# Block 1's gated feed-forward as seven block products a pair, and one packed transpose in the compressed branch

## The chip, the core and the metric

The kernel runs on one core of a Trainium2 chip. The metric is the device time of one execution in microseconds (us), from the first to the last instruction and the little around them. The engines are TensorE (PE in the rows; its weight loads are PEld), VectorE (DVE), ScalarE (ACT), GpSimd (POOL) and SyncE (SP, which here only issues the weight transfers). All work beside each other and meet through semaphores.

## The reference

Three transformer-like blocks run one after the other on 512 tokens of width 1024, in float32. The change touches block 1 only, in two places.

```python
D_MODEL = 1024; SEQ = 512
D_FF = ((8 * D_MODEL // 3 + 255) // 256) * 256          # 2816 = 22 tiles of 128

# feed-forward at the end of block 1
h = rms_norm(x, norm_ffn_g)
x = x + (jax.nn.silu(h @ w_ffn_gate) * (h @ w_ffn_up)) @ w_ffn_down

# compressed branch of the attention: 31 compressed keys, 16 heads, 4 tiles of 128 queries
s_c = jnp.einsum('bgrqd,bgnd->bgrqn', qb, k_c).astype(jnp.float32) * scale
p_c = masked_softmax(s_c, c_end[None, :] <= tpos[:, None])
o_c = jnp.einsum('bgrqn,bgnd->bgrqd', p_c.astype(dt), v_c)
```

## The kernel before

**Products in three parts.** TensorE multiplies in the rounded type fp32r. For float32 accuracy every operand is held as a high half (rounded to fp32r) and a low half (the rest), and a product is three matmuls: high by high, high by low, low by high (`three`, L2553 to L2557). An activation operand is `HI[...]`, `LO[...]`; a weight operand is `w_hi`, `w_lo`.

**Weights as a stream of units.** A unit is 1024 x 128 weights, 512 KB: eight tiles of 128 x 128, one for each slice of the contraction. Every unit U takes the same way through two buffers, by the parity of U: SyncE loads it into `raw` (loop at L400 and behind), ScalarE rounds it into `w_hi` (`split_hi`, L574 to L578, which waits until TensorE has finished unit U - 2), GpSimd subtracts to get `w_lo` (`low_half`, L429 to L431), TensorE runs 24 matmuls of 128 x 512 on it (`unit`, L2569). `PLANS` lists the stages of a block with their units; all engines go through that list in the same order, and semaphores (`w_loaded`, `w_hi_ready`, `w_lo_ready`, `mm_done`) count units.

**The feed-forward.** D_FF is handled in three parts of 8, 8 and 6 tiles. A stage `ffn_up_q` has two units for each tile, one of `w_ffn_gate` and one of `w_ffn_up`: a *pair*, 22 in all. `scaled_pairs` (TensorE, L2612) multiplies, each unit into its own PSUM bank. `scaled_operands` (VectorE, L1702 to L1720) scales the gate by the norm's factor `stat[:, 1]` (L1708), ScalarE applies Silu (L742), VectorE scales up (L1711), multiplies the two (L1714), rounds the hidden tile into its high half (L1718) and subtracts for the low half (L1720). A stage `ffn_down_q` then multiplies the hidden tiles by eight units of `w_ffn_down` (`single`, L2660), and VectorE adds the result to `X` (`residual_add`, L1664). The norm's factor itself comes late: `residual_add_operand` (L1686 to L1696) adds the attention's output to `X` unit by unit in stage `attn_out`, makes the operand (unscaled by the norm) and sums squares; TensorE starts `ffn_up_0` with it before the factor is there (`fresh=True`).

**The compressed branch.** For each head `transposes` (L2853 to L2867) turns four tiles of compressed probabilities (128 queries x 32) with one transpose each (L2862), ScalarE copies them out of PSUM (L975, L976), and `values` (L2882) multiplies each by the compressed values.

## Time and profile before

| | us |
|---|---|
| median of three timed runs | 2816.99 (2815.65 to 2817.27) |
| profiled execution | 2814.94 |
| its span, first to last instruction | 2813.2 |
| TensorE busy | 2719.2 (97%) |
| VectorE / ScalarE / GpSimd busy | 57% / 36% / 42% |
| FFN of block 1 (`ffn_up_0` to `ffn_down_2`) | about 670 to 1048 of the span |

A busy share counts instructions in flight, so for TensorE, whose matmuls overlap, the distance between the starts of two matmuls says more than the share. A row of the timeline gives the start, the duration, the engine, the line, the operation with output and inputs and their shape, and in brackets how long the engine sat idle before it and which engine's instruction ended that. An instruction's duration includes time in which it was started but blocked.

### The profile page before, as it was taken

How to read it: one execution, taken by the hardware profiler on the slowest of the kernel's cores; microseconds unless marked ns; L12 is line 12 of the kernel's file. 1: busy time of each engine (PE TensorE's matmuls, PEld its weight loads, DVE VectorE, ACT ScalarE, POOL GpSimd, SP SyncE). 2: the span in 40 equal slices, each digit the busy share in tenths (PEclk: the TensorE clock that was granted, in tenths of full speed). 3: DMA queues.
4: the chain of work that ended last, by engine and by line, in shares of the span. 5: the costliest groups of instructions: out<-in, count | busy, mean ns of one | idle time of the engine just before them, and what ended most of it. 6: DMA issues, size and time to landing. Idle time of an engine off the chain costs nothing.

```text
span 2813.2 us, 38287 instructions
## 1 busy us (share of the span) xinstructions
PE 2719.2 (97%) x13208; PEld 2244.6 (80%) x13208; DVE 1590.6 (57%) x2560; ACT 1023.4 (36%) x1775; POOL 1178.3 (42%) x592
## 2 busy tenths in 40 slices
PE   8999999999999999999999999999899999999998
PEld 6877888778888877878887788888677778888886
DVE  8996767574433376466665745536623447643364
ACT  4225655533222254443324411112525553211124
POOL 3442585234444443354423344444342214444443
PEclk9999999999999999999999999999999999999999
DMA  3342000132223233222112332232231112322332
GB/s 140 98 135 83 16 24 9 46 127 99 97 93 98 93 120 100 83 87 72 54 38 85 130 101 97 97 96 92 93 105 61 46 45 95 122 97 97 97 97 90
DMA packets 67460, 242.90 MB, mean 86 GB/s; under 512 B 7771, under 2 KB 10116, under 8 KB 66572
## 3 DMA queue, kind: packets, MB, share of 16 engines
q1 hardware_dynamic: 59760, 215.37, 23.3%
q10 hardware_dynamic: 7580, 25.91, 2.6%
q8 instruction: 78, 1.28, 0.2%
q14 instruction: 42, 0.34, 0.0%
HBM read 232.80 MB, written 6.35 MB: 85 GB/s over the span
## 4 chain that ended last, share of the span: by engine, by line
issue 46%; PE 36%; POOL 14%; DVE 2%; ACT 1%; POOLq 0%; DMA 0%; DVEq 0%; SPq 0%; ACTq 0%
POOL w_lo L431 12%; PE bank L2555 9%; PE bank L2557 9%; PE bank L2556 9%; PE bank L3109 2%; PE bank L3098 2%; PE bank L2880 1%; POOL stat L458 1%; POOL stat L455 1%; PE bank L2770 1%; PE bank L2867 0%; PE bank L2741 0%; DVE big L1904 0%; PE bank L2828 0%; PE bank L2829 0%
## 5 line engine op out<-in xcount | busy, mean ns | idle before, releaser
L431 POOL TENSOR_TENSOR w_lo<-raw,w_hi 128x1024 fp32r<-128x1024 f32 x398 | 972.9, 2445 | 1566.5 <-ACT w_hi L578 1446.0
L2555 PE MATMUL bank<-act,w_hi 128*128 128x512 f32 x3128 | 1258.4, 402 | 54.1 <-POOL w_lo L431 16.4
L2557 PE MATMUL bank<-act,w_lo 128*128 128x512 f32 x3128 | 1226.3, 392 | 0.0
L2556 PE MATMUL bank<-act,w_hi 128*128 128x512 f32 x3128 | 1225.0, 392 | 0.0
L2555 PEld LDWEIGHTS bank<-act,w_hi 128*128 128x128 f32 x3128 | 591.5, 189 | 203.4 <-issue 34.6
L578 ACT CAST w_hi<-raw 128x1024 fp32r<-128x1024 f32 x396 | 415.7, 1050 | 906.7 <-PE bank L2557 884.9
L2557 PEld LDWEIGHTS bank<-act,w_lo 128*128 128x128 f32 x3128 | 591.3, 189 | 126.8
L2556 PEld LDWEIGHTS bank<-act,w_hi 128*128 128x128 f32 x3128 | 592.6, 189 | 120.6 <-issue 5.5
L1664 DVE TENSOR_TENSOR X<-X,bank 128x512 f32 x56 | 38.5, 688 | 241.3 <-PE bank L2557 241.3
L2046 DVE CAST act<-tmp 128x512 f32 x64 | 140.9, 2202 | 10.0 <-DVE tmp L2042 5.2
L1816 DVE SCALAR_TENSOR_TENSOR bank<-big,cols,bank 128x512 f32<-128x512 f32 x174 | 117.1, 751 | 0.4
L2880 PE MATMUL bank<-big 128*128 128x64 f32 x640 | 82.1, 276 | 12.9 <-DVE big L1917 12.7
L2880 PEld LDWEIGHTS bank<-big 128*128 128x128 f32 x640 | 77.6, 194 | 17.2 <-issue 14.6
L963 ACT ACTIVATE tmp<-bank,big 128x128 f32<-128x128 f32 (+3 forms) x128 | 66.8, 531 | 41.0 <-DVE big L1904 34.9
L1904 DVE TENSOR_REDUCE big<-bank 128x2 f32<-128x256 f32 (+1 forms) x64 | 52.7, 823 | 45.8 <-PE bank L2830 45.6
L458 POOL TENSOR_TENSOR stat<-stat 128x512 f32<-128x512 f32 x58 | 74.1, 1277 | 4.8
L1711 DVE TENSOR_TENSOR tmp<-bank,stat 128x512 f32<-128x512 f32 x22 | 15.2, 692 | 104.9 <-PE bank L2557 104.9
L973 ACT COPY big<-bank 128x128 f32<-128x128 f32 (+3 forms) x128 | 48.3, 431 | 55.1 <-PE bank L2867 55.0
L2446 DVE SCALAR_TENSOR_TENSOR big<-bank,stat 128x128 f32<-128x128 f32 (+3 forms) x32 | 15.7, 491 | 91.0 <-ACT stat L1389 91.0
L2221 DVE TENSOR_TENSOR stat<-bank,cst 128x256 f32<-128x256 f32 x96 | 40.8, 425 | 39.9 <-PE bank L3098 38.1
L1692 DVE TENSOR_TENSOR X<-X,bank 128x512 f32<-128x512 f32 x24 | 16.5, 688 | 78.8 <-PE bank L2557 73.5
L3098 PEld LDWEIGHTS bank<-big 128*128 128x128 f32 x384 | 50.6, 192 | 12.7 <-ACT big L1199 4.2
(427 smaller groups left out, 2967.3 us busy)
## 6 DMA issues: line engine op xcount, KB each, us to landing
raw<-in_w_dram SPq DMA_DIRECT2D x402, 512.0 KB, 3.5
act_f<-head_rows ACTq DMA_DIRECT2D x8, 768.0 KB, 4.7
proj_rows<-big ACTq DMA_DIRECT2D x4, 1024.0 KB
big<-proj_rows ACTq DMA_DIRECT2D x2, 2048.0 KB, 10.0
X<-in_x_dram SPq DMA_DIRECT2D x4, 512.0 KB, 6.0
act_f<-in_cw1k_dram ACTq DMA_DIRECT2D x4, 512.0 KB, 4.2
cst<-in_consts_dram ACTq DMA_DIRECT2D x2, 648.5 KB, 8.9
X<-big ACTq DMA_DIRECT2D x8, 128.0 KB, 3.2
```

Of the source, the lines that this page charges most:

```text
L431: pool.tensor_tensor(w_lo[:, u], raw[:, u].rearrange("p (k n) -> p k n", k=KT), w_hi[:, u].bitcast(F32), ALU.subtract).then_inc(w_lo_ready, 1)
L458: pool.tensor_tensor(to, acc, product, ALU.add).then_inc(done, 1)
L578: a.copy(w_hi[:, u].rearrange("p k n -> p (k n)"), raw[:, u]).then_inc(w_hi_ready, 1)
L963: a.activation(by_tile(tmp[:, 2 * b + j, 0:kw]), score_branches(n)[:, j], ACT.Exp, bias=MX[:, b, j:j + 1], accum_out=SUMS[:, n % 4, j:j + ...
L1816: v.scalar_tensor_tensor(acc, src, w, acc, ALU.mult, ALU.add).then_inc(conv_tap, 1)
L2046: v.tensor_copy(hi, y).then_inc(hi_made, 1)
L2555: pe.matmul(o, l_hi, r_hi, start=start, stop=False)
L2556: pe.matmul(o, l_hi, r_lo, start=False, stop=False)
L2557: return pe.matmul(o, l_lo, r_hi, start=False, stop=stop)
L2880: pe.matmul(o[:, j], PT[:, b, j, k * P:k * P + P], V_TOK[:, 2 * j + g // 2, k, (g % 2) * DH:(g % 2) * DH + DH], start=k == 0, stop=k == qt)
L3098: ins = pe.matmul(bank[2 + half][:, quad[j]], MT[:, 2 * half + j], TM[:, 2 * half + j], start=True, stop=True)
L3109: ins = pe.matmul(bank[4 + half][:, quad[j]], XM[:, 2 * half + j], UM[h % 2][:, 2 * half + j], start=True, stop=True)
```

## The change

**Seven products.** The pair of gate and up units with its operand is taken as a 2 x 2 block matrix product: rows are gate and up, the contraction is split in slices 0 to 3 and 4 to 7, and the 512 tokens in two halves N1 and N2 of 256. Instead of eight block products (4 slices, 256 tokens, three matmuls each: 12 matmuls of 128 x 256) seven are made. For that:

- A pair's seven weight operands are A11 and A12 (the gate unit, cast and subtracted as before), A22 (half of the up unit) and four sums S_1, S_2, S_4, S_3. VectorE forms the sums (`mix_weights`, four instructions of 512 elements in SBUF), ScalarE rounds A22 and the sums (`split_piece`, five casts of 512), GpSimd makes their low halves (five subtractions of 512). `PIECES = 6` counts them: one whole unit and five halves.
- The operand's mixed forms MIXED_1 to MIXED_4 are made once, in stage `attn_out` (`residual_add_mixed_operand` in place of `residual_add_operand`).
- TensorE writes the products to five banks (A to E); ScalarE keeps the first product in SBUF (`keep_first_product`); VectorE combines the banks to gate and up in seven instructions of 256 elements, and scales.
- The rounding of the hidden tile goes from VectorE to ScalarE (`high_hidden`).
- SyncE loads the next pair's two units once the sums of this pair are made (`loads_behind_pair`). The bytes loaded are the same.
- The adding of `ffn_down_q` is written out, with the first sums of the next stage ahead of its last unit.

**Packed compressed branch.** The four tiles of 32 probabilities a head lie side by side (`PC_ROWS`, 128 x 128) and take one transpose and one copy of 128 columns in place of four transposes and two copies (384 and 128). The values stand in `VC_T` four times, once for each tile at its own 32 rows with zeros elsewhere.

The diff, cut to its core (lines of `@@` name the engine; the semaphore renames and the counters are left out):

```diff
@@ plan and storage @@
     ("attn_out", 8),
-    ("ffn_up_0", 16), ("ffn_down_0", 8), ("ffn_up_1", 16), ("ffn_down_1", 8), ("ffn_up_2", 12), ("ffn_down_2", 8)],
+    ("ffn_up_0", 48), ("ffn_down_0", 8), ("ffn_up_1", 48), ("ffn_down_1", 8), ("ffn_up_2", 36), ("ffn_down_2", 8)],
...
+SEVENTHS = ("ffn_up_0", "ffn_up_1", "ffn_up_2")
+PIECES = 6
...
+        MIXED_1 = HI[B][:, 0:4, N2], LO[B][:, 0:4, N2]
...
+        def slots(F):
+            other = 1 - F % 2
+            return OWN_SLOTS + [(w_hi[:, other, k:k + 4], w_lo[:, other, k:k + 4]) for k in (0, 4)]
+        def split_from(F):
+            return [RAW_W[:, 1 - F % 2, 4:8]] + [SUMS_W[:, n] for n in range(4)]
...
@@ SyncE @@
+def loads_behind_pair(F, L, M, j):
+    sp.wait_ge(weights_mixed, M + 4 * j + 4)
+    for n in range(2):
+        u = (L + n) % 2
+        sp.wait_ge(w_lo_ready, F + PIECES * j + 1 + n)
+        sp.dma_start(raw[:, u], t["w"][L + 2 * j + 2 + n]).then_inc(w_loaded[u], 16)
...
@@ GpSimd @@
+    from_unit = rest + 9
+    for F, L, M, n in SEVEN.values():
+        halves_between(from_unit, F)
+        with pool.Fori(0, n) as j:
+            low_half(F + PIECES * j, F % 2)
+            for k, ((hi, lo), src) in enumerate(zip(slots(F), split_from(F))):
+                pool.wait_ge(w_hi_ready, F + PIECES * j + k + 2)
+                pool.tensor_tensor(lo, src, hi.bitcast(F32), ALU.subtract).then_inc(w_lo_ready, 1)
+        from_unit = F + PIECES * n
+    halves_between(from_unit, heads)
...
@@ ScalarE @@
+def split_piece(stage, j, k):
+    F, L, M, n = SEVEN[stage]
+    if k == 0:
+        a.wait_ge(w_loaded[1 - F % 2], loaded(L, 1) + 16 * j)
+    else:
+        a.wait_ge(weights_mixed, M + 4 * j + k)
+    if isinstance(j, int) and j == 0:
+        if k >= 3:
+            a.wait_ge(mm_done, F)
+    else:
+        a.wait_ge(mm_done, F + PIECES * j - PIECES + SLOT_FREE[k])
+    a.copy(slots(F)[k][0], split_from(F)[k]).then_inc(w_hi_ready, 1)
...
+    def keep_first_product(j, begun=False):
+        a.wait_ge(mm_done, F + PIECES * j + 1)
+        if not begun:
+            a.wait_ge(dve_read, used + 7 * j - 2)
+        a.copy(P1_KEPT, BANK_A).then_inc(act_read, 1)
+    def high_hidden(j):
+        a.wait_ge(full_made, full + j + 1)
+        a.copy(HI[A][:, bass.ds(j, 1), :].rearrange("p a t -> p (a t)"), tmp[:, 3]).then_inc(hi_made, 1)
+    def next_unit(j):
+        u = F % 2
+        a.wait_ge(w_loaded[u], loaded(L, 2) + 16 * j)
+        a.wait_ge(mm_done, F + PIECES * j + 3)
+        a.copy(w_hi[:, u].rearrange("p k n -> p (k n)"), raw[:, u]).then_inc(w_hi_ready, 1)
+    def silu(j):
+        a.wait_ge(gate_scaled, scaled + j + 1)
+        a.activation(tmp[:, 2], tmp[:, 2], ACT.Silu).then_inc(act_read, 1)
+    def rest(j):
+        next_unit(j)
+        for k in range(4):
+            split_piece(name, j + 1, k)
+        silu(j)
+        split_piece(name, j + 1, 4)
...
@@ VectorE @@
+def mix_weights(name, j, k):
+    F, L, M, n = SEVEN[name]
+    first, second = RAW_W[:, F % 2], RAW_W[:, 1 - F % 2]
+    to = SUMS_W[:, k]
+    if k == 0:
+        for x in range(2):
+            v.wait_ge(w_loaded[(L + x) % 2], loaded(L, x) + 16 * j)
+    v.wait_ge(w_lo_ready, F - 1 if isinstance(j, int) and j == 0 else F + PIECES * j - PIECES + k + 3)
+    if k in (1, 2):
+        v.wait_ge(weights_mixed, M + 4 * j + k)
+    one, two = ((second[:, 0:4], second[:, 4:8]), (SUMS_W[:, 0], first[:, 0:4]), (SUMS_W[:, 1], first[:, 4:8]),
+                (first[:, 0:4], second[:, 0:4]))[k]
+    v.tensor_tensor(to, one, two, ALU.add).then_inc(weights_mixed, 1)
...
+def residual_add_mixed_operand(name, block, gain, dst, stage):
...
+        if k < 4:
+            at = made + 2 * k
+            v.tensor_tensor(MIX[:, 4], X[:, k, N1], X[:, k, N2], ALU.subtract).then_inc(full_made, 1)
+            low(LO[dst][:, k, N1], HI[dst][:, k, N1], X[:, k, N1], g(k), at + 1)
+            v.wait_ge(full_made, full + k + 1)
+            low(MIXED_1[1][:, k], MIXED_1[0][:, k], MIX[:, 4], g(k), at + 2)
+        else:
+            i, at, done = k - 4, made + 8 + 4 * (k - 4), full + 4 + 3 * (k - 4)
+            link(v.tensor_scalar(MIX[:, 0], X[:, k, N2], g(k), None, ALU.mult))
+            v.scalar_tensor_tensor(MIX[:, 1], X[:, i, N2], g(i), MIX[:, 0], ALU.mult, ALU.subtract).then_inc(full_made, 1)
+            v.wait_ge(full_made, done + 1)
+            v.scalar_tensor_tensor(MIX[:, 2], X[:, i, N1], g(i), MIX[:, 1], ALU.mult, ALU.subtract).then_inc(full_made, 1)
+            v.wait_ge(full_made, done + 2)
+            v.scalar_tensor_tensor(MIX[:, 3], X[:, k, N1], g(k), MIX[:, 2], ALU.mult, ALU.subtract).then_inc(full_made, 1)
+            low(MIXED_3[1][:, i], MIXED_3[0][:, i], MIX[:, 1], None, at + 2)
+            v.wait_ge(full_made, done + 3)
+            low(MIXED_4[1][:, i], MIXED_4[0][:, i], MIX[:, 3], None, at + 4)
+            low(LO[dst][:, k], HI[dst][:, k], X[:, k], g(k), at + 1)
+            low(MIXED_2[1][:, i], MIXED_2[0][:, i], MIX[:, 2], None, at + 3)
+        if k < KT - 2:
+            add_square(k)
+    mix_weights(stage, 0, 1)
+    add_square(KT - 2)
+    add_square(KT - 1)
+    mix_weights(stage, 0, 2)
+    mix_weights(stage, 0, 3)
...
+    def pair(j, last=False):
+        step = lambda k: v.wait_ge(dve_read, used + 7 * j + k)
+        mix = (lambda k: None) if last else lambda k: mix_weights(name, j + 1, k)
+        mix(0)
+        v.wait_ge(mm_done, F + PIECES * j + 3)
+        v.tensor_tensor(gate[:, N1], BANK_A, r[:, N1], ALU.mult).then_inc(dve_read, 1)
+        mix(1)
+        v.wait_ge(mm_done, F + PIECES * j + 4)
+        v.wait_ge(act_read, reads + 2 * j + 1)
+        v.tensor_tensor(U_PART, P1_KEPT, BANK_B, ALU.subtract).then_inc(dve_read, 1)
+        step(2)
+        v.tensor_tensor(U_PART, U_PART, BANK_C, ALU.add).then_inc(dve_read, 1)
+        mix(2)
+        v.wait_ge(mm_done, F + PIECES * j + 5)
+        step(3)
+        v.tensor_tensor(gate[:, N2], U_PART, BANK_E, ALU.add).then_inc(dve_read, 1)
+        step(4)
+        v.tensor_tensor(gate[:, N2], gate[:, N2], r[:, N2], ALU.mult).then_inc(gate_scaled, 1)
+        mix(3)
+        v.wait_ge(mm_done, F + PIECES * j + 6)
+        v.tensor_tensor(V_PART, BANK_B, P1_KEPT, ALU.subtract).then_inc(dve_read, 1)
+        step(5)
+        v.tensor_tensor(up[:, N1], V_PART, BANK_D, ALU.add).then_inc(dve_read, 1)
+        v.tensor_tensor(up[:, N2], V_PART, BANK_C, ALU.subtract).then_inc(dve_read, 1)
+        step(7)
+        v.tensor_tensor(up, up, r, ALU.mult).then_inc(dve_step, 1)
+        v.wait_ge(dve_step, steps + j + 1)
+        v.wait_ge(act_read, reads + 2 * j + 2)
+        v.tensor_tensor(up, up, gate, ALU.mult).then_inc(full_made, 1)
+        v.wait_ge(full_made, full + j + 1)
+        v.wait_ge(hi_made, made + j + 1)
+        hi = HI[dst][:, bass.ds(j, 1), :].rearrange("p a t -> p (a t)")
+        lo = LO[dst][:, bass.ds(j, 1), :].rearrange("p a t -> p (a t)")
+        v.tensor_tensor(lo, up, hi.bitcast(F32), ALU.subtract).then_inc(lo_made, 1)
...
@@ TensorE @@
+    A11, A12, A22, S_1, S_2, S_4, S_3 = unit_parts + slots(F)
+    B11, B21, B22 = (hi[:, 0:4, N1], lo[:, 0:4, N1]), (hi[:, 4:8, N1], lo[:, 4:8, N1]), (hi[:, 4:8, N2], lo[:, 4:8, N2])
...
+    def product(o, w, x, begin=True, made=None):
+        for k in range(4):
+            if made is not None:
+                pe.wait_ge(lo_made, base + made(k))
+            ins = three(o, w[0][:, k], w[1][:, k], x[0][:, k], x[1][:, k], begin and k == 0, k == 3, skip_group_check=True)
+        return ins
+    def pair(j, begun=False, fresh=False):
+        def piece(k):
+            pe.wait_ge(w_lo_ready, F + PIECES * j + k)
+        def free(k):
+            if not begun:
+                pe.wait_ge(dve_read, used + 7 * j - 7 + k)
+        def fifth():
+            piece(4 if fresh else 3)
+            free(7)
+            product(BANK_C, S_1, MIXED_1, made=(lambda k: 2 * k + 2) if fresh else None)
+        piece(1)
+        free(1)
+        product(BANK_A, A11, B11, made=(lambda k: 2 * k + 1) if fresh else None).then_inc(mm_done, 1)
+        if fresh:
+            fifth()
+        piece(2)
+        free(6)
+        product(BANK_D, A22, MIXED_4, made=(lambda k: 8 + 4 * k + 2) if fresh else None).then_inc(mm_done, 1)
+        pe.wait_ge(act_read, reads + 2 * j + 1)
+        product(BANK_A, A12, B21, begin=False, made=(lambda k: 8 + 4 * k + 3) if fresh else None).then_inc(mm_done, 1)
+        if fresh:
+            sum_squares()
+        else:
+            fifth()
+        piece(4)
+        product(BANK_B, S_2, MIXED_2, made=(lambda k: 8 + 4 * k + 4) if fresh else None).then_inc(mm_done, 1)
+        piece(5)
+        product(BANK_E, S_4, B22).then_inc(mm_done, 1)
+        piece(6)
+        pe.wait_ge(dve_read, used + 7 * j + 2)
+        product(BANK_B, S_3, MIXED_3, begin=False).then_inc(mm_done, 1)
...
@@ compressed branch: TensorE, ScalarE @@
-            for q in range(TT):
-                to = bank[0][:, P + q * P:2 * P + q * P] if q < 3 else bank[6][:, P:2 * P]
-                pe.transpose(to, PC[:, q], ident)
+            pe.transpose(bank[0][:, P:2 * P], PC_ROWS, ident)
...
-        pe.matmul(o[:, 2], PCT[:, h % 2, qt * P:qt * P + P], VC_T[:, g * DH:(g + 1) * DH],
+        pe.matmul(o[:, 2], PCT[:, h % 2], VC_T[:, qt, g * DH:(g + 1) * DH],
...
-            a.copy(PCT[:, h % 2, 0:3 * P], bank[0][:, P:4 * P])
-            a.copy(PCT[:, h % 2, 3 * P:4 * P], bank[6][:, P:2 * P]).then_inc(c_kept, 1)
+            a.copy(PCT[:, h % 2], bank[0][:, P:2 * P]).then_inc(c_kept, 1)
```

What the change moves on three engines, from the instruction streams of both kernels:

VectorE, the loop over the pairs of `ffn_up_0`, before (ISA and REGISTER_ALU are address and counter work of the loop; `tmp` holds gate and up, `stat` the normalising factor):

```order
L1708 TENSOR_TENSOR tmp<-bank,stat 128x512 [waits mm_done]
L1709 REGISTER_ALU
L1710 REGISTER_ALU [waits mm_done]
L1711 TENSOR_TENSOR tmp<-bank,stat 128x512 [waits lo_made]
L1712 REGISTER_ALU
L1713 REGISTER_ALU [waits act_read]
L1714 TENSOR_TENSOR tmp<-tmp 128x512 [waits dve_read]
L1715 REGISTER_ALU
L1718 ISA [waits full_made]
L1718 COPY act<-tmp 128x512
```

The same loop now, its first half (`raw` and `big` in L1885 are weights and weight sums in SBUF, `big<-big,bank` combines a kept product with a PSUM bank):

```order
L1885 TENSOR_TENSOR big<-raw 128x512 [waits w_lo_ready]
L1945 ISA
L1946 TENSOR_TENSOR tmp<-bank,stat 128x256 [waits mm_done]
L1880 REGISTER_ALU
L1882 ISA [waits w_lo_ready]
L1885 TENSOR_TENSOR big<-big,raw 128x512 [waits weights_mixed]
L1948 REGISTER_ALU
L1949 ISA [waits mm_done]
L1950 TENSOR_TENSOR big<-big,bank 128x256 [waits act_read]
L1942 ISA
L1952 TENSOR_TENSOR big<-big,bank 128x256 [waits dve_read]
```

and its end, behind the last product of the pair:

```order
L1963 TENSOR_TENSOR tmp<-big,bank 128x256 [waits dve_read]
L1964 TENSOR_TENSOR tmp<-big,bank 128x256
L1942 REGISTER_ALU
L1966 TENSOR_TENSOR tmp<-tmp,stat 128x512 [waits dve_read]
L1967 REGISTER_ALU
L1968 REGISTER_ALU [waits dve_step]
L1969 TENSOR_TENSOR tmp<-tmp 128x512 [waits act_read]
L1970 REGISTER_ALU
L1971 REGISTER_ALU [waits full_made]
L1974 ISA [waits hi_made]
L1974 TENSOR_TENSOR act<-tmp,act 128x512
```

Five instructions a pair have become fifteen; eight of them read two operands in SBUF (four L1885, L1958 on `tmp` and `stat`, L1966, L1969, L1974). The cast of L1718 has left this engine.

GpSimd, the loop that makes the low halves of these weights. Before, one instruction a unit:

```order
L431 TENSOR_TENSOR w_lo<-raw,w_hi 128x1024 [waits w_hi_ready]
L435 UNCONDITIONAL_BRANCH
L435 ISA
L431 TENSOR_TENSOR w_lo<-raw,w_hi 128x1024 [waits w_hi_ready]
L430 REGISTER_ALU
```

and now, a pair:

```order
L509 TENSOR_TENSOR w_lo<-raw,w_hi 128x1024 [waits w_hi_ready]
L608 REGISTER_ALU
L609 TENSOR_TENSOR big_r<-raw,big_r 128x512 [waits w_hi_ready]
L608 REGISTER_ALU
L609 TENSOR_TENSOR big_r<-big,big_r 128x512 [waits w_hi_ready]
L608 REGISTER_ALU
L609 TENSOR_TENSOR big_r<-big,big_r 128x512 [waits w_hi_ready]
L608 REGISTER_ALU
L609 TENSOR_TENSOR w_lo<-big,w_hi 128x512 [waits w_hi_ready]
L608 REGISTER_ALU
L609 TENSOR_TENSOR w_lo<-big,w_hi 128x512 [waits w_hi_ready]
```

Two instructions of 1024 elements a pair have become one of 1024 and five of 512.

ScalarE, the same loop. Before, the gate's Silu and a weight cast follow one another; now the first rows of an iteration are:

```order
L827 ISA [waits mm_done]
L828 COPY big<-bank 128x256 [waits dve_read]
L831 REGISTER_ALU
L832 ISA [waits full_made]
L832 COPY act<-tmp 128x512
L836 ISA
L837 REGISTER_ALU [waits w_loaded_odd]
L838 CAST w_hi<-raw 128x1024 [waits mm_done]
```

The cast of the next pair's weights (L838) stands behind L832, which waits for VectorE's last but one instruction of the pair before (`full_made`).


## Rows read from the trace of the kernel before

**Rows 1.** The page: busy time of each engine, share of the span, instructions.
```profile
PE 2719.2 (97%) x13208; PEld 2244.6 (80%) x13208; DVE 1590.6 (57%) x2560; ACT 1023.4 (36%) x1775; POOL 1178.3 (42%) x592
```

**Rows 2.** Busy time in the stretch of `ffn_up_1`; columns length, PE, PEld, DVE, ACT, POOL.
```profile
801.00:889.00 88.00, 88.00 (x390) 72.87 (x389) 42.63 (x42) 21.05 (x24) 40.91 (x17) 1.00 0.29 96
```

**Rows 3.** Timeline (start, duration, engine, line, operation, idle before): two pairs of `ffn_up_0`.
```profile
700.66 0.69 DVE L1711 TENSOR_TENSOR tmp<-bank,stat 128x512 f32<-128x512 f32 x1 [4.84 <-PE bank L2557]
...
701.39 0.69 DVE L1714 TENSOR_TENSOR tmp<-tmp 128x512 f32<-128x512 f32 x1
...
701.71 2.63 POOL L431 TENSOR_TENSOR w_lo<-raw,w_hi 128x1024 fp32r<-128x1024 f32 x1 [1.80 <-ACT w_hi L578]
...
702.22 2.40 DVE L1718 CAST act<-tmp 128x512 f32 x1
...
711.54 0.69 DVE L1711 TENSOR_TENSOR tmp<-bank,stat 128x512 f32<-128x512 f32 x1 [4.84 <-PE bank L2557]
```

**Rows 4.** Timeline: matmuls of 256 columns in a stream, and the four small transposes, in the attention.
```profile
338.50 0.60 PE L2862 MATMUL bank<-cst,big 128*128 128x128 f32 x4
338.94 0.38 PE L2867 MATMUL bank<-cst,tmp 128*128 128x128 f32 x2
...
339.62 0.28 PE L2828 MATMUL bank<-act,big_r 128*128 128x256 f32 x1
339.73 0.28 PE L2829 MATMUL bank<-act,big_r 128*128 128x256 f32 x1
339.85 0.28 PE L2830 MATMUL bank<-big_r 128*128 128x256 f32 x1
339.96 1.22 PE L2880 MATMUL bank<-big 128*128 128x64 f32 x10
```

**Rows 5.** Timeline: VectorE and GpSimd side by side in stages `conv_out` and `attn_out`.
```profile
587.69 2.39 POOL L431 TENSOR_TENSOR w_lo<-raw,w_hi 128x1024 fp32r<-128x1024 f32 x1 [4.23 <-ACT w_hi L578]
587.71 2.92 DVE L1995 TENSOR_TENSOR big<-big,X  x1
...
620.66 0.69 DVE L1995 TENSOR_TENSOR big<-big,X  x1
...
644.83 2.43 POOL L431 TENSOR_TENSOR w_lo<-raw,w_hi 128x1024 fp32r<-128x1024 f32 x1 [3.02 <-ACT w_hi L578]
...
644.91 0.69 DVE L1487 TENSOR_TENSOR bank<-bank,tmp 128x512 f32<-128x512 f32 x1
```

**Rows 6.** Groups of instructions by line and shape: count, busy us, mean ns, idle before.
```profile
L458 POOL TENSOR_TENSOR stat<-stat 128x512 f32<-128x512 f32 x58 | 74.1, 1277 | 4.8
L490 POOL TENSOR_TENSOR stat<-stat,big 128x512 f32<-128x512 f32 x7 | 7.4, 1052 | 0.5
L2221 DVE TENSOR_TENSOR stat<-bank,cst 128x256 f32<-128x256 f32 x96 | 40.8, 425 | 39.9 <-PE bank L3098 38.1
L578 ACT CAST w_hi<-raw 128x1024 fp32r<-128x1024 f32 x396 | 415.7, 1050 | 906.7 <-PE bank L2557 884.9 <-DMA raw<-in_w_dram 11.6 <-issue 9.4
L827 ACT CAST act<-big 128x512 fp32r<-128x512 f32 x8 | 4.9, 616 | 9.1 <-DVE big L1741 8.9
```

**Rows 7.** Timeline: the last unit of `attn_out` on VectorE, and the norm's factor behind it.
```profile
665.40 0.69 DVE L1692 TENSOR_TENSOR X<-X,bank 128x512 f32<-128x512 f32 x1 [3.48 <-PE bank L2557]
...
667.27 0.75 DVE L1696 SCALAR_TENSOR_TENSOR act<-X,cols,act 128x512 fp32r<-128x512 f32 x1
...
673.28 0.69 DVE L1708 TENSOR_TENSOR tmp<-bank,stat 128x512 f32<-128x512 f32 x1 [1.55 <-ACT stat L603]
```

**Rows 8.** Timeline of TensorE where `ffn_down_0` waits for its last hidden tile.
```profile
759.30 0.39 PE L2557 MATMUL bank<-act,w_lo 128*128 128x512 f32 x1
759.90 0.50 PE L2555 MATMUL bank<-act,w_hi 128*128 128x512 f32 x1 [0.21 <-DVE act L1720]
```

**Rows 9.** Busy time in a stretch of the attention, columns as in rows 2.
```profile
300.00:450.00 150.00, 144.29 (x1052) 132.05 (x1053) 99.64 (x284) 84.30 (x266) 123.08 (x116) 0.99 0.05 15
```

**Rows 10.** Busy time at the end of the attention; the column behind POOL is the granted TensorE clock.
```profile
515.00:520.00 5.00, 3.53 (x18) 3.37 (x18) 2.49 (x7) 0.00 (x0) 1.75 (x1) 0.61 0.32 105
```

246 lines of the change are left out of this document (203 added, 43 removed).

## Prediction

> **What bounds the kernel now.** I read the page first: TensorE is busy 97% of the span, no other engine over 57% [rows 1]. The busy time in stretches says the same of the stages that change: 88.0 of 88.0 us in `ffn_up_1`, with VectorE at 43 and GpSimd at 41 [rows 2]. The timeline gives the step. L1711 reads the up unit of a pair at 700.66 and of the next at 711.54: a pair takes 10.88 us, which over its 48 matmuls of 512 columns is 226.7 ns each [rows 3]. So these stages are bound by matmuls, and fewer matmul columns are worth time exactly as long as no other engine needs more than the new TensorE time for a pair.
>
> **TensorE's side.** Matmuls of 256 columns start at 339.62, 339.73, 339.85 and 339.96, so 113 ns apart [rows 4]: half of 226.7, nothing is lost by halving. A pair becomes 7 x 12 x 113 ns = 9.5 us, 1.36 us less, and over 22 pairs 30 us could be won.
>
> **The other engines for one pair.** GpSimd has one subtraction of 1024 at 2.39 alone [rows 5] and five of 512. None of 512 on weights stands in the trace; L458, two plain operands, took 1.28, L490, with one operand repeated, 1.05 [rows 6]. I take 1.28, since these operands are plain too: 2.39 + 5 x 1.28 = 8.8 us. That alone would fit in 9.5. ScalarE: 1.05 for the unit, six casts of 512 at 0.62 [rows 6], and as an estimate 0.4 and 0.6 for the kept product (256) and Silu (512), 5.8 us: it fits. VectorE: seven instructions of 512 at 0.69, eight of 256 at 0.42 [rows 3, 6], 8.2 us, and 0.04 to 0.14 us between two of them in a loop (701.39 starts 0.04 behind the end of L1711, 702.22 starts 0.14 behind that of L1714 [rows 3]), so 9 to 10 us: just about TensorE's new time.
>
> **But VectorE and GpSimd exclude each other.** This is the row on which the forecast rests. L1995 adds two SBUF operands. Alone it took 0.69; begun 0.02 us behind a GpSimd subtraction of 2.39 it took 2.92, and ended 0.55 us behind it [rows 5]. An add with one PSUM operand, begun 0.08 behind such a subtraction, took its 0.69 [rows 5]. The other way round, the subtraction begun at 701.71 beside L1714 took 2.63 in place of 2.39 and ended 2.26 behind L1714's end [rows 3]. The cast L1718 was blocked as well, 2.40 us, in every pair [rows 3]; it goes to ScalarE, so one victim leaves. Eight new or remaining ones stand in the pair: four weight sums, gate by factor (256), up by factor, up by gate, the low half. What each holds exclusively is the time that it ended behind the other: 0.55 for 512 elements, so 0.28 for 256; on GpSimd 2.26 and, less the same 0.13 at the start, 1.15. The sum is 2.26 + 5 x 1.15 + 7 x 0.55 + 0.28 = 12.1 us a pair. **That is more than the 10.88 of today.** Before, the two engines had one such blocked stretch in 10.88 us and it cost nothing, since TensorE did not wait for it.
>
> The Trainium skill, "SBUF — State Buffer", section "Who interferes with whom", says that VectorE's second read port is GpSimd's only one, that it is taken for a whole instruction, and that a VectorE instruction with two SBUF inputs, but not one with a single one, contends with a GpSimd instruction that reads SBUF. By that rule, the trace agrees in both directions, and the rule speaks against this change.
>
> **The steady pair.** 12.1 needs the port never idle. It will be idle, for the engines also wait in a ring. ScalarE's program puts the cast of the next pair's unit behind `high_hidden`, which waits for up by gate of the pair before. From one up by gate to the next: the high half 0.62 and the unit's cast 1.05 (1.7); GpSimd's six subtractions, 8.8, between which VectorE gets three of its weight sums and the gate's scaling in, 3 x 0.55 + 0.28 = 1.9; then up by factor, blocked behind GpSimd's last one, 0.55, and up by gate, 0.69. Sum 13.6, and 0.2 for the hand-overs: **13.8 us a pair**, 2.9 more than before. From both sides: 12.1 by the port alone; 15.0 if VectorE's gaps of up to 0.14 fall on the ring each time. I take 13.8, as the ring is written so in the program and the gap of 0.04 is as frequent as that of 0.14. TensorE then works 9.5 of 13.8 us.
>
> 22 pairs x 2.92 = 64 us. The first pair of a stage finds its weights made in the stage ahead, and the last makes none for a successor; I take 1.2 us off for each of these six: **+57 us** (bounds +20 and +85).
>
> **Around the pairs.** In `attn_out` VectorE's work for each of the last four units grows: the add 0.69, one scaling of 0.3, six instructions of 256 at 0.42, one of 512 at 0.75, the sum of squares 0.69, so 5.0 us, eight of them with two SBUF operands, and in each unit of 5.44 us (24 x 226.7 ns) GpSimd holds the port for 2.4. VectorE so falls some 2 us a unit behind, 8 us at the last, where before its last low half was done under 3 us behind the last add's start (665.40 to 668.0), and the factor was applied at 673.28 [rows 7]. TensorE's first two products need only the first four slices and cover 2.3 us. I take **+7 us**, bounds 2 and 15.
>
> At the start of each `ffn_down`, the cast of its second unit stands behind the last `high_hidden`. From the last product on: five VectorE instructions 2.6 and gaps 0.3, the high half 0.62, the cast 1.05, GpSimd 2.40 and one blocked 0.55, so 7.5 us, against the 5.44 us that the first down unit takes. That is 2 us of waiting in place of the about 0.4 of today (759.30 to 759.90, less one step of 0.23 [rows 8]): three times 1.7, **+5 us**, bounds 0 and 8. Within the down stages I cost the written-out add at nothing: it is one add of 0.69 in 5.44 us, and the four sums before the last one (2.8 us, up to 5 if blocked) still end within a unit.
>
> In the attention TensorE is busy 144.3 of 150 us [rows 9]. Four small transposes take 338.50 to 338.94, 0.11 us each [rows 4]; three of four go, for 16 heads: 48 x 0.11 = **-5 us**, bounds 0 and -8 (ScalarE is also relieved of a copy a head).
>
> **Sum.** 57 + 7 + 5 - 5 = +64 us on the profiled execution's 2814.9, so 2879. The median of the timed runs stands 2.1 us above that execution: 2881.
>
> **The rivals.**
>
> *A, the ring at the shared port (the forecast), slower.* 12.1 to 15.0 us a pair, with the other terms at their ends: +24 to +104, 2841 to 2921. Chance 0.73.
>
> *B, the block costs less than its sum*, because GpSimd's short subtractions leave gaps which VectorE uses without a loss, or take 1.05. Then VectorE's own work bounds, 10.3 us a pair: 22 x -0.6 = -13, + 7 + 5 - 5: about 2811, between 2800 and 2830. For it: GpSimd's 1.05 exists [rows 6]. Against it: every overlap of two SBUF operands that I looked at was a full block. Chance 0.10.
>
> *C, the other side: faster.* All three helpers stay below TensorE's 9.5 us a pair, 22 x -1.36 = -30, + 7 + 3 - 5: 2792. It decides itself where port and ring together come to less than 9.5 us; by the sum above they miss this by 2.6. It holds if the instructions that VectorE issues now do not need GpSimd's port, as the one with a PSUM operand did not [rows 5]. Chance 0.09.
>
> *D, TensorE's clock.* With gaps in every pair the granted clock may fall. Where TensorE was busy 3.5 of 5 us in the attention's end the grant was 0.61 [rows 10]: for most of that stretch the lower level, 1.2 GHz. If some 3 us of every second pair ran so, 1.5 us each would be added, 11 x 1.5 = 16, and more in `attn_out`: 2895 to 2940. For it: 9.5 of 13.8 us is no higher a share than 3.5 of 5. Against it: products wait singly, never for much over 2 us. Chance 0.08.
>
> That the change does less than it says can be left aside: the instruction streams show all seven products and one transpose a head.
>
> **How the numbers follow.** The likeliest case is A, 2881. For 8 in 10 I need A and a part of D, and a little of B: 2830 to 2925. Outside are C, most of B and the top of D. A measurement of this kernel can tell about 0.2%, 5.6 us, from no change. Faster by more: C and a third of B, 0.12. Within: 0.05. Slower: A, D and the rest, 0.83.
>
> **What would show it.** Right: the starts of the first matmul of two pairs lie 12.1 to 15 us apart; weight sums (L1885) average well over 0.69 and some 1.5 us or more; GpSimd's 512 subtractions average over 1.28; TensorE is busy about 70% in `ffn_up_1`, waiting mostly for VectorE reading a bank or for GpSimd's low halves. Wrong: pairs at 9.5 to 10.9 us, weight sums at 0.69 beside a running subtraction. The attention should be 5 us shorter, and the wait ahead of the first gate scaling some 7 us longer. I would be wrong in size if the ring is cut, for instance if ScalarE's cast of the next unit finds `full_made` long reached.

## The result, and the profile after

The changed kernel takes **2896.4 us** (median), the kernel before 2816.8 us beside it: ratio 1.0285, 95% interval 1.0267 to 1.0303, so 80 us slower. 2881 was predicted, with a range of 2830 to 2925. The profiled execution has a span of 2893.2 us against 2813.2. All ratios here are of undisturbed executions; one of a later kernel (copies and operands in PSUM) took 8088 us in the slow state and is left out of its ratio.

The busy time of the whole span on the page, then a stretch of 112 us over `ffn_up_1`, which before took 88 us [rows 2]; its columns are start and end, length, then busy time of PE, PEld, DVE, ACT and POOL, granted clock, DMA share, GB/s:

```profile
PE 2724.6 (94%) x13952; PEld 2284.2 (79%) x13952; DVE 1772.4 (61%) x2816; ACT 1084.6 (37%) x1908; POOL 1290.1 (45%) x680
...
832.00:944.00 112.00, 90.85 (x674) 88.35 (x673) 91.65 (x114) 42.20 (x69) 80.28 (x47) 0.92 0.22 76
```

Before, TensorE never stopped there [rows 2]. Now it is idle for 21 of 112 us, while VectorE is busy for 92 (43 before) and GpSimd for 80 (41). VectorE's work by line, from 675 to 1070 us of the changed kernel (busy us, mean ns, then idle time ahead of the group and what ended it):

```profile
L1885 DVE TENSOR_TENSOR big<-raw 128x512 f32<-128x512 f32 x43 | 63.7, 1482 | 14.0 <-DMA raw<-in_w_dram 12.2 <-ACT stat L698 1.8
L1885 DVE TENSOR_TENSOR big<-big,raw 128x512 f32<-128x512 f32 x43 | 58.8, 1367 | 0.4
L1966 DVE TENSOR_TENSOR tmp<-tmp,stat 128x512 f32<-128x512 f32 x21 | 33.7, 1606 | 0.7
L1958 DVE TENSOR_TENSOR tmp<-tmp,stat 128x256 f32<-128x256 f32 x21 | 21.2, 1010 | 0.7
...
L1974 DVE TENSOR_TENSOR act<-tmp,act 128x512 f32 (+1 forms) x21 | 14.5, 693 | 19.1 <-ACT act L832 19.1
...
L1950 DVE TENSOR_TENSOR big<-big,bank 128x256 f32<-128x256 f32 x21 | 8.7, 415 | 16.4 <-PE bank L2883 16.4
```

The weight sums (L1885), two SBUF operands, average 1.37 and 1.48 us where 0.69 is their own time; the two scalings (L1966, L1958) 1.61 and 1.01 where 0.69 and 0.42 would do. The low half (L1974) has two SBUF operands as well but took 0.69: GpSimd was idle by then. All that read a bank, as L1950, took their plain 0.41 to 0.42. GpSimd in the same stretch:

```profile
L509 POOL TENSOR_TENSOR w_lo<-raw,w_hi 128x1024 fp32r<-128x1024 f32 x38 | 94.9, 2501 | 132.8 <-ACT w_hi L838 81.0 <-ACT w_hi L673 51.8
L609 POOL TENSOR_TENSOR big_r<-big,big_r 128x512 fp32r<-128x512 f32 x43 | 69.2, 1630 | 4.6 <-ACT big_r L789 4.6
L609 POOL TENSOR_TENSOR w_lo<-big,w_hi 128x512 fp32r<-128x512 f32 x44 | 64.0, 1469 | 6.5 <-ACT w_hi L789 6.5
```

Its subtractions of 512 take 1.47 to 1.63 in place of 1.28. And this is whom TensorE waited for from 625 to 1130 us (total, times, longest; the four largest):

```profile
PE bank L2881 <- DVE tmp L1963: 37.2, 19, 2.7
PE bank L2881 <- DVE big L1950: 18.0, 10, 3.1
PE bank L2881 <- POOL big_r L609: 10.9, 1, 10.9
PE bank L2881 <- POOL w_lo L509: 7.8, 6, 3.0
```

The period of a pair shows in the first bank read, L1946. One row gives the eight of `ffn_up_0` (duration in ns as smallest, median and largest, then the first and the last start):

```profile
L1946 DVE TENSOR_TENSOR tmp<-bank,stat x8: 416/418/420, 685.2 to 782.4; 128x256 f32<-128x256 f32 x8
```

Seven intervals in 97.2 us are 13.9 us each, where the kernel before had 10.88 [rows 3]. "Interval" below is always this mean over the seven intervals of `ffn_up_0`. The last of the seven is shorter, since the last pair makes no sums for a successor: 12.9 us here against 14.0 in the mean of the other six, and in later kernels down to 7.9. Where that misleads, the text says so.

Where the 80 us of span went, by TensorE's first matmul of each stage in both traces: up to `attn_out` -4.0; `attn_out` +1.6; `ffn_up_0`, `_1`, `_2` +34.3, +24.9, +19.2 (some 9.4 of the first belong to its first pair, which waits 10.9 us for GpSimd); the starts and ends of the three down stages +1.1, +1.1, +4.0; the rest -2.2.

### The profile page after: what moved, and what is told of

Read it like the earlier page. It is cut to its first block, busy times and chain, and to the rows that moved or that the text cites. A ratio compares the mean times of both kernels' runs of the same rounds, so it can differ in the third digit from the quotient of the medians.

```text
span 2893.2 us, 41013 instructions
## 1 busy us (share of the span) xinstructions
PE 2724.6 (94%) x13952; PEld 2284.2 (79%) x13952; DVE 1772.4 (61%) x2816; ACT 1084.6 (37%) x1908; POOL 1290.1 (45%) x680
## 3 DMA queue, kind: packets, MB, share of 16 engines
q8 instruction: 80, 1.31, 0.2%
## 4 chain that ended last, share of the span: by engine, by line
issue 48%; PE 32%; POOL 17%; DVE 2%; ACT 1%; POOLq 1%; DMA 0%; DVEq 0%; SPq 0%; ACTq 0%
POOL w_lo L509 11%; PE bank L2881 8%; PE bank L2883 7%; PE bank L2882 7%; POOL big_r L609 2%; POOL w_lo L609 2%; PE bank L3494 2%; PE bank L3483 2%; PE bank L3265 1%; POOL stat L544 1%; POOL stat L541 1%; PE bank L3157 0%; PE bank L3252 0%; DVE big L1885 0%; DVE big L2218 0%
## 5 line engine op out<-in xcount | busy, mean ns | idle before, releaser
L509 POOL TENSOR_TENSOR w_lo<-raw,w_hi 128x1024 fp32r<-128x1024 f32 x376 | 918.0, 2442 | 1519.3 <-ACT w_hi L673 1317.8
L2881 PE MATMUL bank<-act,w_hi 128*128 128x512 f32 (+1 forms) x3040 | 1200.8, 395 | 60.6 <-POOL w_lo L509 21.7
L2883 PE MATMUL bank<-act,w_lo 128*128 128x512 f32 (+1 forms) x3040 | 1168.1, 384 | 0.0
L2882 PE MATMUL bank<-act,w_hi 128*128 128x512 f32 (+1 forms) x3040 | 1167.2, 384 | 0.0
L2881 PEld LDWEIGHTS bank<-act,w_hi 128*128 128x128 f32 x3040 | 581.6, 191 | 195.5 <-issue 34.4
L673 ACT CAST w_hi<-raw 128x1024 fp32r<-128x1024 f32 x352 | 369.6, 1050 | 820.0 <-PE bank L2883 808.9
L2882 PEld LDWEIGHTS bank<-act,w_hi 128*128 128x128 f32 x3040 | 581.3, 191 | 107.5 <-issue 5.5
L3265 PEld LDWEIGHTS bank<-big 128*128 128x128 f32 x640 | 76.6, 192 | 19.5 <-issue 15.5
L2881 PE MATMUL bank<-big_r 128*128 128x256 f32 x176 | 55.8, 317 | 37.2 <-DVE tmp L1963 37.2
L1885 DVE TENSOR_TENSOR big<-raw 128x512 f32<-128x512 f32 x44 | 65.5, 1489 | 14.0 <-DMA raw<-in_w_dram 12.2
L609 POOL TENSOR_TENSOR big_r<-big,big_r 128x512 fp32r<-128x512 f32 x44 | 70.6, 1624 | 5.9 <-ACT big_r L789 5.9
L2881 PEld LDWEIGHTS bank<-big_r 128*128 128x128 f32 x176 | 36.9, 210 | 41.4 <-DVE tmp L1963 41.2
```

The lines of the kernel that those rows point to most:

```text
L509: pool.tensor_tensor(w_lo[:, u], raw[:, u].rearrange("p (k n) -> p k n", k=KT), w_hi[:, u].bitcast(F32), ALU.subtract).then_inc(w_lo_ready, 1)
L609: pool.tensor_tensor(lo, src, hi.bitcast(F32), ALU.subtract).then_inc(w_lo_ready, 1)
L673: a.copy(w_hi[:, u].rearrange("p k n -> p (k n)"), raw[:, u]).then_inc(w_hi_ready, 1)
L1885: v.tensor_tensor(to, one, two, ALU.add).then_inc(weights_mixed, 1)
L2881: pe.matmul(o, l_hi, r_hi, start=start, stop=False, **group)
L2882: pe.matmul(o, l_hi, r_lo, start=False, stop=False, **group)
```

## Experiments

My theory was the prediction's: VectorE and GpSimd exclude each other when VectorE has two SBUF operands, and the pair's period is a ring through these blocked instructions. Rivals: VectorE's own in-order work, the port being simply full, the clock, or one more ring.

### The packed compressed branch alone

```
the kernel before, with  PCT = region(2 * P),  VC_T with a copy of the values for each quarter,
one pe.transpose of PC_ROWS a head; the feed-forward untouched
```

> The kernel before with the packed compressed branch alone, full result. From the two traces: the attention and what lies ahead of it ended 4.0 us earlier after the change, and nothing else of this part touches the feed-forward. Theory: 2816.8 - 4 = 2812.8 us (ratio 0.9986). Rival: the 4 us come from elsewhere (VectorE's shorter attention, another order of the weight loads), then no change, 2816.8.

Measured: 2811.2 us against 2815.7, ratio 0.9985 (0.9976 to 0.9994). The stretch of the attention from 272 to 520 us in this run:

```profile
272.00:520.00 248.00, 230.02 (x1692) 209.43 (x1691) 174.91 (x491) 138.63 (x439) 141.55 (x130) 0.99 0.06 18
```

The kernel before has 1724 matmuls there and 233.03 us, 1692 and 230.03 in the changed kernel. This half of the change is worth -4.6 us as a kernel by itself; the rest of the 80 us, some 84, is the other half's.

### Four of the eight operands into PSUM

```diff
-                gate, up, r = tmp[:, 2], tmp[:, 3], stat[:, 1]
+                gate, up, r = tmp[:, 2], bank[7], stat[:, 1]
+                gate_2 = bank[6][:, S // 2:S]
```

> The changed kernel with up, and the second half of gate, kept in PSUM; full result. Four VectorE instructions of a pair (gate by factor, up by factor, up by gate, the low half) then have only one operand in SBUF. Theory (port shared with GpSimd, and the ring through it): 3 x 0.55 + 0.28 = 1.9 us a pair leave the ring, 14.1 becomes 12.2 to 12.6, the whole 2896 - 22 x 1.7 = 2858 us, and the blocked durations of these four fall from 1.6, 0.8, 0.7 us to their own 0.69 and 0.42. Rival, VectorE's own in-order time bounds or TensorE's waits for its banks bound: the number and the sizes of the instructions are unchanged, so the pair stays at 14.0 us and the whole at 2894.

```profile
L1885 DVE TENSOR_TENSOR big<-raw 128x512 f32<-128x512 f32 x43 | 67.5, 1570 | 31.4 <-DMA raw<-in_w_dram 29.7 <-ACT stat L698 1.8
...
L1967 DVE TENSOR_TENSOR bank<-bank,stat 128x512 f32<-128x512 f32 x22 | 15.4, 700 | 0.8
```

2874.1 us, 22 less; interval 12.4 in place of 13.9. Up by factor fell from 1.61 to 0.70 us, as theory had it, but the gain is 1.0 us a pair and not 1.7. (The interval flatters it: its last is 9.25 us, and the other six have a mean of 13.0, also 1.0 less than before the edit.) The first row above shows one reason: VectorE now waits 29.7 us for weight loads (12.2 in the changed kernel). Another is on ScalarE: its cast of the next unit waited for TensorE 9 times in the changed kernel and 19 times here, in each case from 690 to 1072 us:

```profile
ACT w_hi L838 <- PE bank L2883: 9.3, 9, 1.3
ACT w_hi L838 <- PE bank L2884: 13.8, 19, 1.1
```

Other things came late as soon as this was early.

### The cast ahead of the high half

```diff
                 def rest(j):
                     next_unit(j)
+                    high_hidden(j - 1)
...
                     v.tensor_tensor(gate[:, N1], BANK_A, r[:, N1], ALU.mult).then_inc(dve_read, 1)
                     mix(1)
+                    low_hidden(j - 1)
```

> The changed kernel with two instructions in another order, full result: ScalarE casts the next pair's unit before the high half of the hidden row, and VectorE's low half of pair j-1 stands behind the second weight sum of pair j. The work on every engine and at the port is the same. Theory (ring, as in the prediction): GpSimd's first subtraction starts without waiting for up by gate, the ring falls by 0.62 and by what of the 1.05 of the cast now lies beside VectorE's tail; 12.5 to 13.2 us a pair, 2896 - 22 x 1.3 = 2868 us. Rival, the port itself is full: nothing is taken from it, the pair stays at 14.0 and the whole at 2894. Rival, the moved low half now delays the sums and the bank reads behind it: slower than 2896.

```profile
L1886 DVE TENSOR_TENSOR big<-raw 128x512 f32<-128x512 f32 x42 | 63.4, 1511 | 40.0 <-DMA raw<-in_w_dram 27.9 <-issue 10.8 <-ACT stat L698 1.4
...
L1947 DVE TENSOR_TENSOR act<-tmp,act 128x512 f32 (+1 forms) x19 | 31.6, 1663 | 4.8 <-ACT act L832 4.8
```

2907.6 us: 11 slower where 28 faster was expected. Three things are seen. The low half, 0.69 us while GpSimd was idle, stands behind the second sum now and takes 1.66. The sums wait 27.9 us for loads. And the cast that was to come earlier now waits for TensorE, 47.0 us in 17 of 20 cases, since it overwrites the weights of the third product (`mm_done`):

```profile
ACT w_hi L838 <- PE bank L2892: 47.0, 17, 4.5
```

**The ring of the prediction is not the only one.** The changed kernel's own timeline shows a second and a third (start, length):

```profile
848.44 1.77 DVE L1885 TENSOR_TENSOR big<-raw 128x512 f32<-128x512 f32 x1
...
850.51 0.92 SPq L487 DMA_DIRECT2D raw<-in_w_dram  x2
...
851.37 1.41 DVE L1966 TENSOR_TENSOR tmp<-tmp,stat 128x512 f32<-128x512 f32 x1
852.90 0.69 DVE L1969 TENSOR_TENSOR tmp<-tmp 128x512 f32<-128x512 f32 x1
853.74 0.62 ACT L832 CAST act<-tmp 128x512 f32 x1 [2.60 <-DVE tmp L1969]
854.30 1.05 ACT L838 CAST w_hi<-raw 128x1024 fp32r<-128x1024 f32 x1
...
855.43 2.40 POOL L509 TENSOR_TENSOR w_lo<-raw,w_hi 128x1024 fp32r<-128x1024 f32 x1 [3.20 <-ACT w_hi L838]
...
855.55 2.82 DVE L1885 TENSOR_TENSOR big<-raw 128x512 f32<-128x512 f32 x1 [0.32 <-DMA raw<-in_w_dram]
...
865.73 0.39 PE L2881 MATMUL bank<-big_r 128*128 128x256 f32 x1 [2.15 <-DVE tmp L1963]
866.32 0.41 PE L2882 MATMUL bank<-big_r 128*128 128x256 f32 x1
866.53 0.41 PE L2883 MATMUL bank<-big_r 128*128 128x256 f32 x1
...
868.47 0.62 ACT L832 CAST act<-tmp 128x512 f32 x1 [2.59 <-DVE tmp L1969]
870.40 1.05 ACT L838 CAST w_hi<-raw 128x1024 fp32r<-128x1024 f32 x1 [1.31 <-PE bank L2883]
```

In the first pair shown two chains leave the fourth sum's end at 850.21. One goes over VectorE's tail, the high half and the unit's cast to GpSimd's start at 855.43. The other goes over the load of the next two units: issued 850.51, since the fourth sum is the last reader of their buffers, landed by 855.5, when the first sum starts. They are equally long to 0.1 us, so a cut in one gives little. In the next pair a third chain ends last: VectorE's read of bank D (L1963) releases TensorE's second product at 865.73, and the unit's cast waits for the end of the third, until 870.40, 1.31 us behind the high half. TensorE runs at its lower clock there (matmuls 0.21 us apart, where 0.12 is usual).

### Both edits, and half of the loads

> Both edits of the two runs ahead: up and half of gate in PSUM, and the cast of the next unit ahead of the high half; full result. Port's sum by the prediction's terms 12.1 - 1.9 = 10.2 us, ring cut. Theory: 10.5 to 11.5 us a pair, 2896 - 22 x 3.1 = 2828 us, still not under the 2816.8 of before. Rival, if one edit already did all (they cut the same wait): 12.4 us a pair, 2860. If seven products could win at all, the pair would come under 10.88.

2884.9 us, interval 13.2: 57 us over the expected 2828 and 11 worse than the first edit alone, as the new order cost 11 us in the run ahead too. The blocked low half is not what costs this: it takes 0.68 us here. The sums wait 46.2 us for loads, and the unit's cast waits for TensorE in 19 cases, 45.9 us. The next two runs load half of each unit inside the loops (stale weights in the other half), on the changed kernel and on this one:

```diff
-                    sp.dma_start(raw[:, u], t["w"][L + 2 * j + 2 + n]).then_inc(w_loaded[u], 16)
+                    sp.dma_start(raw[:, u, 0:4 * P], t["w"][L + 2 * j + 2 + n][:, 0:4 * P]).then_inc(w_loaded[u], 16)
```

> The changed kernel, but in the loops over pairs each weight load brings only the first 512 of a unit's 1024 columns; the others keep stale weights, so the products' numbers are others. Question: is there a second ring through the loads (fourth weight sum, load issued, 5.0 us to the landing, first sum), as long as the one of the prediction (fourth sum, up by factor, up by gate, high half, unit's cast)? In the trace after, sum four ended 850.21, the loads were issued 850.51, and the next pair's first sum waited for the landing until 855.55, while ScalarE's unit cast, behind the high half, ended 855.35. Theory, twin rings of the same length: the load's half alone wins little, 14.1 becomes 13.8 to 14.0, and with shorter first pairs the whole is 2896 - 6 = 2890 us. Rival, the loads alone bound: 2.4 us less a pair, 2843. Rival, no ring of loads: 2895.

> The kernel with up and half of gate in PSUM and the unit's cast moved ahead of the high half (2884.9 us, pairs of 12 and 15.6 us, VectorE waiting 46 us for loads), and half loads as before (stale weights in the other half). Theory, twin rings: here the ring over the high half is cut and the loads are what is left; with half of the load time gone the pair falls to 11 to 12 us, 2885 - 22 x 2.0 = 2841 us, much more than the same edit gives in the run beside this one. Rival, the port or VectorE's own time bounds: 2880.

Measured 2891.2 us (-5, interval 13.6) and 2840.5 us (-44, interval 11.3), each a single run. What the edit does to a load, issue to landing from 690 to 780 us in the changed kernel (KB each, median us), first whole, then half:

```profile
raw<-in_w_dram SPq DMA_DIRECT2D x14, 512.0 KB, 3.9
raw<-in_w_dram SPq DMA_DIRECT2D x14, 256.0 KB, 2.8
```

The same edit gives over eight times as much where the other order was in. So the loads alone do not bound the changed kernel, and they do stand in the second one. Two limits: the changed kernel's runs spread over 8 us, so its -5 does not by itself tell 2890 from the 2895 of no ring. And the -44 is more than the loads' own part: an interval is 1.9 us shorter, a load 1.1 (both loads together some 1.4), and the four sums, which now stand less behind GpSimd's subtractions, took 1.4 us less a pair (means 1.32 to 1.05 and 1.71 to 1.28). The loads matter there also by when the sums start.

### The weight sums off the port

```diff
+                if apart:
+                    two = bank[7].rearrange("p (k n) -> p k n", k=4)
                 v.tensor_tensor(to, one, two, ALU.add).then_inc(weights_mixed, 1)
```

> The changed kernel with the second operand of the weight sums of pairs 2 to n-1 read from a bank that holds zeros: the sums are of the same size and in the same places, but have one operand in SBUF (numbers of the products are others). Theory, port: the sums' durations fall from 1.4 mean to 0.69 and GpSimd's subtractions from 1.5 to 1.3 or less; 4 x 0.55 = 2.2 us leave the ring; 16 of the 22 pairs have it: 14.1 becomes 12.0 to 12.6, 2896 - 16 x 1.8 = 2867 us. Rival, the block is not what sets the pair (VectorE's issue and order, TensorE's waits): durations fall, the pair stays at 14, 2893 us.

```profile
L1887 DVE TENSOR_TENSOR big<-big,bank 128x512 f32<-128x512 f32 x32 | 21.7, 678 | 0.0
```

2837.3 us (a single run), interval 11.0, and 10.4 in the steady part: twice the expected gain, from 16 pairs. The sums stand ahead of the fourth sum's end, from which all the chains leave, and there they count with their whole length. In the pair from 855.55 on they took 2.82, 1.42, 0.99 and 1.76 us, 7.0 in all; unblocked they are 2.7. The difference of 4.3 us is somewhat more than the 3.6 by which a steady pair fell (14.0 to 10.4). The block is the cause; that it costs most ahead of the reload is my reading of the timeline, no run changes the loads' place alone.

### The clock

```diff
+                        for _ in range(16):
+                            pe.matmul(bank[1][:, 0:S // 2], HI[B][:, 0, 0:P], HI[B][:, 0, N1], start=True, stop=True, skip_group_check=True)
                     free(6)
```

> The changed kernel with 16 matmuls of 256 columns into an unused bank ahead of the second product of every pair but the first of a stage: 16 x 0.113 = 1.8 us in the wait of 2.2 us there. It tells what the fallen clock costs (granted 0.91 and 0.95 in the up stages, against 0.98 and more before; about one half-rate stretch of 3.4 us in each pair). Theory: TensorE is not what the pair waits for, the clock rises to 0.98 and the time stays within 4 us of 2896. Rival, the slow products sit in the ring: 0.5 to 1 us a pair, 2874 to 2885. Rival, the dummy matmuls themselves delay product two: 2900 or more.

2892.2 us, a single run, 4.3 less; the changed kernel's runs themselves spread over 8. The interval is 13.6 in place of 13.9. From 783 to 940 us the granted clock rose from 0.95 to 0.98, from 672 to 783 us from 0.91 to 0.98, first this run, then the changed kernel:

```profile
672.00:783.00 111.00, 99.19 (x776) 95.52 (x777) 92.65 (x115) 43.53 (x70) 79.00 (x46) 0.98 0.22 77
```

```profile
672.00:783.00 111.00, 86.53 (x631) 83.86 (x632) 88.53 (x114) 43.56 (x70) 74.77 (x46) 0.91 0.22 81
```

So rival D's mechanism is there: in 12 of the 22 pairs of the changed kernel some 3 us of matmuls came 0.21 us apart, the lower clock of 1.2 GHz, much as D supposed. What it costs is small and not told apart from the spread: 4 us by this run, not 16 or more. Where it costs is seen on ScalarE, whose cast of the unit now hardly waits for TensorE (9.3 us in 9 cases before):

```profile
ACT w_hi L839 <- PE bank L2884: 1.6, 2, 0.8
```

### A repair with the full result

ScalarE has time to spare. It copies the halves of the raw weights into idle banks, and the sums read one operand there:

```diff
+                    a.copy(KEPT[k], by_2(raw[:, u, half * S:half * S + S])).then_inc(raw_copied, 1)
...
+                    two = KEPT[(0, 1, 2, 1)[k]]
```

> The changed kernel with full result: in the loops over pairs ScalarE copies three halves of the raw weights into idle banks (3 x 0.62 us more on it, 7.7 in all), and VectorE's four weight sums read one operand there. In the run with zeros in a bank the pair took 10.4 us (2837.3 us in all). Theory, the sums' blocking stands in both rings: here the same, and one copy of 0.62 ahead of the first sum: 10.7 to 11.3 us a pair, the whole 2837 + 16 x 0.6 = 2847 us. Rival, ScalarE becomes the bound (its casts of the slices now come 1.9 us later and GpSimd waits for each): 12.5 us a pair, 2873 us. Rival, the short time with zeros came from elsewhere (no dependence of the sums on the loads): 13.5 to 14 us, 2890.

> Both: the weight sums from copies in banks, and up and half of gate in PSUM, so that none of VectorE's eight instructions in a pair's loop has two SBUF operands; full result. Theory: what is left is GpSimd's own 2.4 + 5 x 1.28 = 8.8 us, TensorE's 9.5, ScalarE's 7.7 and hand-overs: 9.7 to 10.4 us a pair, under the 10.88 of before for the first time. Whole: 2847 - 22 x 0.8 = 2829 us, since the stages' beginnings (first pairs' wait for loads, about 3 us each, attn_out and the first pair 11 us, down starts 6 us) stay as they are; so slower than before still, by 0.3 to 0.6%. Rival, the loads (5.0 us from issue to landing, behind the fourth sum) then bound alone: 10.9 us a pair, 2845.

2848.9 us (interval 11.4) and, with up and half of gate in PSUM too, 2825.6 us, ratio 1.0036 (1.0020 to 1.0051). Both within 4 us of what was expected. VectorE and GpSimd in the second:

```profile
L1907 DVE TENSOR_TENSOR big<-raw,bank 128x512 f32<-128x512 f32 x38 | 25.9, 683 | 39.3 <-ACT bank L854 39.3
```

```profile
L611 POOL TENSOR_TENSOR w_lo<-big,w_hi 128x512 fp32r<-128x512 f32 x44 | 56.9, 1317 | 1.3 <-ACT w_hi L791 1.3
```

```profile
L1969 DVE TENSOR_TENSOR tmp<-bank,stat x8: 415/418/419, 685.8 to 756.5; 128x256 f32<-128x256 f32 x8
```

Sums at 0.68, GpSimd's subtractions at 1.32, an interval of 10.1 us: under 10.88, for the first time a pair of seven products is shorter. What bounds it is TensorE again, busy 40.0 of 40 us, with VectorE at 30 and GpSimd at 34:

```profile
830.00:870.00 40.00, 40.00 (x334) 39.99 (x333) 29.57 (x60) 28.23 (x49) 34.23 (x25) 1.00 0.31 105
...
707.04 0.28 PE L2906 MATMUL bank<-big_r 128*128 128x256 f32 x1
707.16 0.28 PE L2904 MATMUL bank<-big_r 128*128 128x256 f32 x1
707.28 0.28 PE L2905 MATMUL bank<-big_r 128*128 128x256 f32 x1
```

In a long stream the matmuls of 256 columns start 0.120 us apart, not the 0.113 of [rows 4]: 84 of them are 10.1 us. So seven products with matmuls at this step take 10.1 us and not 9.5, 0.8 under before, and 22 pairs could win 17.6 us and not 30. Yet the kernel is still slower than before, by what stands at the stages' edges: 10.8 us in the first pair, 3.0 at the last down stage's start.

The next run changes three orders there:

```diff
-                        piece(4 if fresh else 3)
+                        piece(3)
...
+                split_hi(F + PIECES * n + 1, (F + PIECES * n + 1) % 2)
                 high_hidden(n - 1)
...
                     for k in range(5):
+                        if k == 3:
+                            keep_first_product(0, True)
                         split_piece(name, 0, k)
```

> The kernel of the run before (pairs of 10.15 us, 2825.6 us in all) with three changes of order at the stages' edges, full result. (1) The first pair of ffn_up_0: the fifth product waits only for the second slice's low half and no longer for the third's; TensorE's wait of 10.8 us there should fall to 6 to 7. (2) ScalarE casts the second down unit as soon as the last product is done, ahead of the last high half; TensorE's wait for that unit's low half, 3.0, 1.3 and up to 3.0 us, goes. (3) In ffn_up_1 and ffn_up_2 the first product is copied aside ahead of the casts of the last two slices; 1.9 us each go. Theory, these waits are on the path: -4, -6 and -4 us, 2811 to 2813 us, faster than before by 0.1% and level with the packed compressed branch alone (2811.2), so the seven products then cost and win nothing. Rival, each wait is followed by another that comes just as late (rstd, the bank reads of VectorE): 2820 or more. Rival, the earlier cast delays the high half: down starts longer than now.

2814.2 us, ratio 0.9996 (0.9987 to 1.0005): no change to the kernel before is shown, and 1 us over what was expected. TensorE's waits in it:

```profile
PE bank L2906 <- DVE big L1975: 10.4, 4, 4.2
PE bank L2906 <- POOL big_r L611: 5.0, 1, 5.0
```

The 10.8 fell to 5.0 and the down starts are mended, but the 1.9 us ahead of the third product came back as 3.0 and 2.9 ahead of the seventh: VectorE's reads of the first pair stand behind sums that wait for the next load. So the last run puts them ahead of these sums, and gives the first pairs' sums copies in banks too:

```diff
-                    mix(0)
+                    if not first:
+                        mix(0)
                     v.wait_ge(mm_done, F + PIECES * j + 3)
...
+        KEPT_0 = by_2(bank[3]), by_2(bank[7]), by_2(bank[6])
```

> The kernel of the run before (2814.2 us) with the first pair of each stage changed, full result. In its trace VectorE's first weight sum for pair two waits for the loads (5.1 us to 811.41, 4.2 us to 682.08) with the bank reads of pair one behind it, and TensorE waits 3.0, 2.9 and 4.2 us for one of these reads. (1) In the first pair the first two sums for the next one come behind the first three bank reads. (2) For ffn_up_1 and ffn_up_2 the sums of the first pair too, in the down stage ahead, read copies in idle banks: their chain (2.4, 1.6, 1.6 and 1.8 us) falls to some 3.5 us, and with it the next loads are issued up to 3.5 us earlier. Theory: TensorE then waits only for pair two's first low half (until 684.0 in ffn_up_0): -1.5 there and -3 to -4 in the other two, 2805 to 2808 us, under the 2811.2 of the packed compressed branch alone and 0.3% under the kernel before. Rival, what sets the second pair is the chain load, cast, low half, which (1) leaves where it is and (2) moves less than thought: 2811 to 2814, nothing won. Rival, the copies delay ScalarE's casts of the first slices: over 2815.

```profile
PE bank L2924 <- POOL big_r L612: 5.0, 1, 5.0
PE bank L2924 <- POOL w_lo L512: 4.4, 4, 2.3
PE bank L2924 <- DVE bank L2005: 3.9, 3, 1.4
```

**2809.8 us, ratio 0.9972 (0.9961 to 0.9982): faster than before**, 4.4 us less than the run ahead where 6 to 9 were expected (6.8 by the ratios, as the kernel before ran 1.7 us slower beside it); the wait of 10.4 became 3.9, that for the low halves grew from 2.0 to 4.4. Against the packed branch alone (0.9985, 0.9976 to 0.9994, on another chip) the intervals overlap: that the seven products in this form win anything is not shown, only that they need cost nothing.

## Why the prediction was right, point by point

- **TensorE bound before, no longer after.** Right: 91 of 112 us busy in `ffn_up_1`, though that is 81% and not the 70% named, as the matmuls took longer than counted.
- **TensorE's side, 9.5 us a pair.** Wrong, without harm to the forecast, as TensorE did not bind. "Nothing is lost by halving" was read from four starts; over whole pairs a matmul of 256 columns takes 0.120 us and a pair 10.1. The gain on offer was 17.6 us, not 30. Why it is 0.120 no run shows.
- **The port.** Right, and the experiments show it as the cause: taking the operands off the port took the interval from 13.9 to 10.1, where TensorE binds, with not one instruction of VectorE or GpSimd fewer, and ScalarE with three more.
- **The steady pair, 13.8 us.** Measured 13.9, and 13.6 to 14.2 in the middle of a stage. The value came out, but the reason was a part of it, and that the number fits so well is in part luck: a second ring, over the loads, is as long, and a third, over TensorE's third product, ended last in 9 of 21 casts. In only 10 of the 21 did the cast follow straight behind the high half, as the prediction has it. It had costed neither the load nor that wait. The changed kernel holds `raw` until the fourth sum, and two units need 5.0 us from issue to landing. By the prediction alone, moving the cast should have won 28 us; it lost 11.
- **Price of a block.** 0.55 for each instruction fits the ring through GpSimd, whose own time is in the sum. In the ring over the loads the first sum costs 2.82, as it stands behind all of the 2.40 us subtraction. The rule I drew from the one overlap in the trace of before [rows 5] was right, the use of it too narrow.
- **First and last pairs, 1.2 off for each of six.** Half wrong. The last interval of a stage is 12.9, 1.2 less. The first saves little: in `ffn_up_1` it took 14.65 and the one behind it 12.4, as the next pair's loads are issued only behind its sums. With 22 x 3.1 less 3 x 1.2 the pairs come to about +65, where +57 was taken; the three stages gained 78, less the 9.4 of the next point: +69.
- **`attn_out` and the first pair, +7.** Measured 1.6 + 9.4 = 11, inside the bounds of 2 and 15. The first gate scaling started at 685.2 where it had been 673.3, 12 us later and not some 7. Part of it was no cost of the scheme: the fifth product waited for one slice too many, and undoing that took the wait from 10.8 to 5.0.
- **Down starts, +5.** Measured +6.2, but as 1.1, 1.1 and 4.0 where three times 1.7 was taken: the sum fits better than its terms. TensorE waited 1.4 us for the second unit's low half at the first start and 3.0 at the last.
- **Attention, -5.** Measured -4.0 in the traces, -4.6 as a kernel by itself.
- **Rivals.** B and C needed the blocks to be small or absent, and they were not. With them gone the pair was at 10.1, near B's 10.3 but bound by TensorE and not by VectorE; C's 9.5 a pair was out of reach, since the matmuls alone take 10.1. D's clock fell, to 0.91, in about as many pairs as D supposed, and cost some 4 us at most by a single run, not 16.
- **The bounds of A.** "+24 to +104, with the other terms at their ends" does not follow from the terms: +20, +2, 0 and -8 make +14, and +85, +15, +8 and 0 make +108. The measured +80 lies inside either.
- **The Trainium skill**, "SBUF — State Buffer", section "Who interferes with whom", carried the forecast together with [rows 5]: it says that a VectorE instruction with two SBUF inputs contends with a GpSimd instruction that reads SBUF, and one with a single such input does not. This case's runs agree with it in both directions: two SBUF operands 1.37 to 1.61 us, the same instruction with one operand in a bank 0.68 to 0.70, and GpSimd's subtraction 1.63 down to 1.34.

## What to carry to other kernels

An algebraic saving on TensorE moves its price to the engines that form the sums, and there the count of instructions tells less than where their operands lie: before adding VectorE work with two SBUF operands beside a busy GpSimd, see whether one of them can stand in PSUM, even at the price of a ScalarE copy. When a loop falls behind, look for every chain from one iteration to the next, the reload of a buffer by its last reader among them; if cutting one chain wins little and a wait for another releaser grows, there are two or more of about one length, and a cut in what they share pays most. Measure the step of the smaller matmul in a stream as long as the new loop's before counting the saving: 7 ns of 113 took 0.6 us of the expected 1.36 a pair. And short stages pay for their first and last iteration each time: 22 pairs at up to 0.8 us less each were eaten by three edges until these were mended.

## What was not expected of the hardware

- A copy of 128x512 from SBUF to a bank took ScalarE 0.58 us, beside both other engines at work, and a sum with that operand 0.68: the two together are less than the blocked sum's 1.4.
- An instruction's price depends on its place: the low half took 0.69 us at the pair's end, with GpSimd idle, and 1.66 behind the next pair's second sum.
- In a long stream TensorE's matmuls of 256 columns started 0.120 us apart, those of 512 columns 0.227; its weight loads were then in flight 39.99 of 40 us, against 72.87 of 88 with 512 columns [rows 2].
- The granted clock was 0.91 in `ffn_up_0` with waits of 2 to 3 us in each pair, 0.98 with 16 dummy matmuls in one of the waits, and 1.00 once TensorE no longer waited.
